# A transformer block stack on one core: the first mixer's columns in another order, and its selector's work in other places

## The chip, the cores and the metric

The kernel runs on one core of a Trainium2 chip. The metric is the device time of one execution in microseconds (us), median of repeated runs. PE is TensorE (its weight loads are PEld), DVE is VectorE, ACT is ScalarE, POOL is GpSimd, SP is the queue that issues the DMAs.

## What is computed

256 tokens of width 1024 pass two layers of a first kind (a SwiGLU network, a hybrid mixer, a SwiGLU network) and two of a second kind. The change touches the hybrid mixer only, which runs twice. One projection with 3792 columns feeds three attentions:

```python
proj = u @ w_in                     # 3792 columns, split into:
# aq ak av | iq ik iw | bq bk bv | cq ck cv | cf cg
aq, ak = rope(rms_norm(aq)), rope(rms_norm(ak))          # A: 4 heads, one shared key/value head
iq, ik = rope(iq), rope(ik)                              # selector: 8 heads, one key
score  = sum_h iw_h * scale * relu(iq_h . ik)            # causal
sel    = top_64(score)                                   # A attends to these keys only
bq, bk = rope(rms_norm(bq)), rope(rms_norm(bk))          # B: 4 heads, plain causal here (one block)
cq, ck = rms_norm(cq), rms_norm(ck)                      # C: 8 heads, forget gate
log_f  = log_sigmoid(cf + forget_bias)                   # cumulated over tokens, added to C's scores
o_c    = o_c * sigmoid(cg)
out    = concat(o_a, o_b, o_c) @ w_out
```

## The kernel before

Every engine runs a program written out by hand; semaphores join them. No planner is at work: what stands first in an engine's program runs first, and a waiting instruction holds all that stand behind it.

All weights come as a stream of parts of up to 128x2048 floats, three in flight. For each part ACT makes a rounded copy `w_hi` (`split_hi`, L330), which waits until the part three before it is used up, and DVE makes the rest `w_lo` (`split_lo`, L337). PE multiplies with both (L523 to L525).

In the first mixer (`mixer1`, written once for each engine) the 3792 columns are 15 parts, numbered m = 0 to 14: eight column groups g = 0 to 7, each of two halves in depth but for the last. `project_group` does a part for the first 128 tokens, then calls `within_part(m)`, does the second 128 tokens, and `after_part(m)` follows. So small work of the attentions stands between halves and parts of the projection. ACT and DVE have their own `within_part` and `after_part`, and their splits of part m + 3 stand in their `after_part(m)`. When a group is complete, `evacuate` (ACT, L1329) brings it from PSUM to `proj` (`proj_ready`).

The chain of the selector: POOL rotates its queries `I_Q` and key `I_K` (`rope1`, `rope_ready`), PE transposes them (`qk_turn`, L842), ACT copies them out (`qk_copy`, `qkT_ready`), PE multiplies (`index_scores`, L855, eight units u of two heads), ACT takes `relu(u)`, DVE weights and sums (`add_index(u)`, L1947, `idx_used`). `relu(u)` waits for `add_index(u - 2)`, since two buffers alternate. Then DVE searches in 8 rounds of `top_rounds` for each half of the tokens (L1962, L1963), and A's scores need the mask (`mask_ready`).

Norms of heads: ACT squares (`group_squares`, L1343), DVE sums (`head_means`, L1922, `gmean`), POOL takes the root (`group_roots`, L2316, `groot`), DVE scales (`scale_heads`, L1929; C's signal is `cqk_ready`) and, for A and B, applies gains (`gain_heads`, L1936, `normed`). The forget gate: DVE makes `z_abs`, ACT an exponential and a logarithm, DVE `log_f` (`logf_ready`), PE cumulates it (L912), ACT and DVE take it over (`forget_terms`).

The eight attention batches (C, C, A, B; two halves of tokens each) pass PE `scores(i)`, DVE `maxima(i)` (L1893), ACT `weights(i)` (L1313), PE `turn_p(i)` (L815), DVE `turned_p(i)`, PE `weigh(i)` (L826), DVE `weighed(i)` (`o_ready`). `turn_p(i)` also waits for `o_ready` of batch i - 1. At the end PE transposes the results (L702) and `project_out` multiplies by `w_out`.

## Time and profile before

| | |
|---|---|
| median of 3 runs | 1916.12 us (1915.83 to 1916.45) |
| the profiled execution | 1916.21 us, span of its trace 1914.1 us |
| PE busy | 1894.2 us, 99% |
| DVE, ACT, POOL busy | 1337.4, 968.3, 151.6 us |

Busy time on PE counts modelled ends, which reach over the next start: back to back, 128x512 matmuls start every 0.23 us but are shown with 0.39 us. An idle time in brackets is therefore a little shorter than what a wait takes from the flow of starts. A row's bracket names what ended the idle time before it.

### The profile page before, as it was taken

Reading aid. Unit: us, or ns where it says so; the run is one execution under the profiler, and the core shown is the slowest. Engines: PE = TensorE matmul, PEld = TensorE weight load, DVE = VectorE, ACT = ScalarE, POOL = GpSimd, SP = SyncE. Lnnn points to the kernel's source line nnn. Section 1 sums busy time; section 2 is a strip of 40 time slices with the busy share of each in tenths; the row PEclk is TensorE's granted clock in tenths of the full one; section 3 lists DMA queues with packets and bytes.
Section 4 is the critical chain, followed back from the end, with each engine's and each line's share of the span. In section 5 each row is a group of like instructions: output and inputs, shape, how many; then the busy total and the mean of one; then the engine's idle time right before and its main releaser. Section 6 shows DMA issues by size and latency. Waiting matters only on the chain.

```text
span 1914.1 us, 26132 instructions
## 1 busy us (share of the span) xinstructions
PE 1894.2 (99%) x10940; PEld 1639.4 (86%) x10940; DVE 1337.4 (70%) x1469; ACT 968.3 (51%) x1216; POOL 151.6 (8%) x158
## 2 busy tenths in 40 slices
PE   9999999999999999999999999999999999999998
PEld 7888878888888888788888888888888888888887
DVE  7887687787678766868776555569765654569763
ACT  5444565544444445555444565455444665455442
POOL 0000422100000005111000110000000110000000
PEclk9999999999999999999999999999999999999999
DMA  7655532455555555334545443444555443445552
GB/s 283 209 186 181 194 118 109 154 198 177 180 199 193 178 196 187 118 110 155 197 168 194 150 168 134 174 176 170 193 182 186 135 160 141 162 177 184 179 182 104
DMA packets 47491, 327.28 MB, mean 171 GB/s; under 512 B 5520, under 2 KB 5520, under 8 KB 11536
## 3 DMA queue, kind: packets, MB, share of 16 engines
q1 hardware_dynamic: 46512, 323.25, 47.4%
q10 hardware_dynamic: 864, 2.38, 0.3%
q8 instruction: 86, 1.41, 0.3%
q14 instruction: 29, 0.24, 0.0%
HBM read 324.56 MB, written 1.05 MB: 170 GB/s over the span
## 4 chain that ended last, share of the span: by engine, by line
PE 94%; DVE 3%; ACT 1%; issue 1%; POOL 1%; DMA 0%; DVEq 0%; POOLq 0%; ACTq 0%
PE ps L535 34%; PE ps L537 17%; PE ps L523 9%; PE ps L525 9%; PE ps L524 9%; PE ps L529 2%; PE ps L826 2%; PE ps L781 1%; PE ps L783 1%; PE ps L782 1%; PE ps L792 1%; PE ps L530 1%; PE ps L815 1%; DVE w_lo L337 1%; PE ps L550 1%
## 5 line engine op out<-in xcount | busy, mean ns | idle before, releaser
L330 ACT CAST w_hi<-raw 128x2048 fp32r<-128x2048 f32 (+3 forms) x314 | 580.2, 1849 | 581.9 <-PE ps L537 353.4
L337 DVE TENSOR_TENSOR w_lo<-raw,w_hi 128x2048 fp32r<-128x2048 f32 (+3 forms) x314 | 699.3, 2229 | 245.7 <-ACT w_hi L330 242.9
L535 PE MATMUL ps<-x_hl,w_hi 128*128 128x512 f32 x1968 | 494.2, 393 | 0.0
L535 PEld LDWEIGHTS ps<-x_hl,w_hi 128*128 128x128 f32 x1968 | 353.7, 189 | 63.6
L537 PEld LDWEIGHTS ps<-x_hl,w_lo 128*128 128x128 f32 x1968 | 268.5, 190 | 19.3
L537 PE MATMUL ps<-x_hl,w_lo 128*128 128x256 f32 x1968 | 274.4, 282 | 0.0
L523 PE MATMUL ps<-w_hi,x_hl 128*128 128x512 f32 (+3 forms) x672 | 262.0, 390 | 0.0
L525 PE MATMUL ps<-w_hi,x_hl 128*128 128x512 f32 (+3 forms) x672 | 254.2, 378 | 0.0
L524 PE MATMUL ps<-w_lo,x_hl 128*128 128x512 f32 (+3 forms) x672 | 253.5, 377 | 0.0
L1785 DVE TENSOR_REDUCE ffn_tmp<-ps 128x512 f32<-128x1024 f32 x132 | 161.3, 1223 | 103.5 <-PE ps L537 102.8
L535 PE MATMUL ps<-hid_hl,w_hi 128*128 128x512 f32 x836 | 212.9, 394 | 0.0
L535 PEld LDWEIGHTS ps<-hid_hl,w_hi 128*128 128x128 f32 x836 | 149.4, 188 | 26.9
L525 PEld LDWEIGHTS ps<-w_hi,x_hl 128*128 128x128 f32 x672 | 126.3, 188 | 23.5
L523 PEld LDWEIGHTS ps<-w_hi,x_hl 128*128 128x128 f32 x672 | 126.6, 188 | 22.3 <-issue 1.4
L524 PEld LDWEIGHTS ps<-w_lo,x_hl 128*128 128x128 f32 x672 | 126.7, 189 | 20.1
L2312 POOL TENSOR_TENSOR stat<-stat,const 128x2 f32<-128x2 f32 (+1 forms) x15 | 25.7, 1712 | 1448.9 <-DVE stat L1686 821.9
L537 PEld LDWEIGHTS ps<-hid_hl,w_lo 128*128 128x128 f32 x836 | 115.3, 188 | 10.3
L537 PE MATMUL ps<-hid_hl,w_lo 128*128 128x256 f32 x836 | 118.2, 282 | 0.0
L1201 ACT ACTIVATE x_hl<-h,gains 128x256 fp32r<-128x256 f32 x80 | 39.0, 507 | 91.3 <-DVE h L1868 78.4
L1242 ACT ACTIVATE ffn_tmp<-ffn_tmp 128x512 f32<-128x512 f32 x66 | 41.8, 633 | 71.1 <-DVE ffn_tmp L1791 70.8
L1245 ACT CAST hid_hl<-ffn_tmp 128x512 fp32r<-128x512 f32 x66 | 41.0, 621 | 25.0 <-DVE ffn_tmp L1796 24.1
L529 PE MATMUL ps<-x_hl,w_hi 128*128 128x512 f32 x144 | 51.5, 400 | 0.0
(286 smaller groups left out, 2198.4 us busy)
## 6 DMA issues: line engine op xcount, KB each, us to landing
raw<-in_parts SPq DMA_DIRECT2D x278, 1024.0 KB, 4.8
raw<-in_parts SPq DMA_DIRECT2D x20, 768.0 KB, 4.2
raw<-in_parts SPq DMA_DIRECT2D x4, 928.0 KB, 4.6
raw<-in_parts SPq DMA_DIRECT2D x4, 864.0 KB, 4.4
raw<-in_parts SPq DMA_DIRECT2D x6, 512.0 KB, 3.8
raw<-in_parts SPq DMA_DIRECT2D x4, 576.0 KB, 3.9
const<-in_const ACTq DMA_DIRECT2D x1, 1093.0 KB, 5.3
h<-in_x_t SPq DMA_DIRECT2D x1, 1024.0 KB, 7.6
```

Of the source, the lines that this page charges most:

```text
L330: nc.scalar.copy(w_hi[:, i % RING, 0:n_of(i)], raw[:, i % RING, 0:n_of(i)]).then_inc(high_ready, 1)
L337: nc.vector.tensor_tensor(w_lo[:, s, 0:n], raw[:, s, 0:n], w_hi[:, s, 0:n].bitcast(F32), ALU.subtract).then_inc(low_ready, 1)
L523: nc.tensor.matmul(out_, a_hi, b_hi, start=start, stop=False, skip_group_check=True)
L524: nc.tensor.matmul(out_, a_hi, b_lo, start=False, stop=False, skip_group_check=True)
L525: return nc.tensor.matmul(out_, a_lo, b_hi, start=False, stop=stop, skip_group_check=True)
L529: nc.tensor.matmul(ps[:, bank, :], w_h, hl.rearrange("p x n -> p (x n)"), start=start, stop=False, skip_group_check=True)
L535: nc.tensor.matmul(ps[:, bank, :], w_h(c), hl(c).rearrange("p x n -> p (x n)"), start=start and c == 0, stop=False, skip_group_check=True)
L537: m = nc.tensor.matmul(ps[:, bank, 0:SEQ], w_l(c), hl(c)[:, 0, :], start=False, stop=stop and c == kc - 1, skip_group_check=True)
L1201: nc.scalar.activation(x_hi(c), h[:, c, :], ACT.Copy, scale=gains[:, s, c:c + 1]).then_inc(xhi_ready, 1)
L1242: nc.scalar.activation(g_tmp, g_tmp, ACT.Silu).then_inc(silu_ready, 1)
L1245: nc.scalar.copy(hid_hl[:, p - 1:p + 1, 0, :], u_tmp.rearrange("p (f n) -> p f n", f=2)).then_inc(hidhi_ready, 1)
L1785: return nc.vector.tensor_reduce(dst.rearrange("p (f n) -> p f n", f=2), ps[:, b:b + 2, :].rearrange("p b (x n) -> p b n x", x=2), AX_X, A ...
```

## The change

The columns are laid out anew. Before, the groups were C_Q; I_Q; A_Q, A_K, A_V, I_K, I_W, C_F; C_K; C_V; B_Q, B_K; C_G; B_V. Now C_Q stands third: I_Q; A_Q to C_F; C_Q; C_K; C_V and so on. The work of the selector, of the norms and of the forget gate is placed to other parts accordingly on every engine, the search is spread as two rounds over each of eight places, and squares of heads go into a buffer of their own (`squares_early`) instead of `ffn_tmp`. Near the mixer's end the transposes of C's gated result come after `scores(5)` instead of ahead of it, and three small pieces stand one place earlier within `project_out`.

```diff
-MIX1 = (("C_Q", 1736, 512), ("I_Q", 384, 512), ("A_Q", 0, 256), ("A_K", 256, 64), ("A_V", 320, 64), ("I_K", 896, 64),
-        ("I_W", 960, 8), ("C_F", 3272, 8), ("C_K", 2248, 512), ("C_V", 2760, 512), ("B_Q", 968, 256), ("B_K", 1224, 256),
+MIX1 = (("I_Q", 384, 512), ("A_Q", 0, 256), ("A_K", 256, 64), ("A_V", 320, 64), ("I_K", 896, 64),
+        ("I_W", 960, 8), ("C_F", 3272, 8), ("C_Q", 1736, 512), ("C_K", 2248, 512), ...
-WIN1 = column_parts([512, 512, 464, 512, 512, 512, 512, 256])
+WIN1 = column_parts([512, 464, 512, 512, 512, 512, 512, 256])
...
-        QK_UNITS = [((12, 13), ("cqk_ready", 1), 0), ((14, 15), ("cqk_ready", 1), 1), ((3, 4), ("rope_ready", 1), 2),
-                    ((5, 6), ("rope_ready", 1), 3), ((7,), ("rope_ready", 2), 0), ((16, 17), ("cqk_ready", 2), 2),
-                    ((18, 19), ("cqk_ready", 2), 1), ((0, 1), ("rope_ready", 3), 3), ((2,), ("rope_ready", 3), 3),
+        QK_UNITS = [((3, 4), ("rope_ready", 1), 2), ((5, 6), ("rope_ready", 1), 3), ((7,), ("rope_ready", 2), 0),
+                    ((12, 13), ("cqk_ready", 1), 1), ((14, 15), ("cqk_ready", 1), 0), ((0, 1), ("rope_ready", 3), 1),
+                    ((2,), ("rope_ready", 3), 0), ((16, 17), ("cqk_ready", 2), 2), ((18, 19), ("cqk_ready", 2), 3),
```

PE, the new `within_part`, then `after_part`:

```diff
+                    if m == 5:
+                        qk_turn(2)
+                    if m == 6:
+                        index_scores(2, 3)
+                    if m == 7:
+                        index_scores(6, 7)
                     if m == 9:
                         pe.wait_ge(S["relu_ready"], 8)
                         qk_turn(7)
                         qk_turn(8)
+                    if m >= 10:
+                        turn_p(m - 10)
...
                     if m == 4:
                         qk_turn(0)
+                        qk_turn(1)
                     if m == 5:
+                        pe.wait_ge(S["qkT_ready"], 3)
+                        index_scores(0, 1)
                         pe.wait_ge(S["logf_ready"], 1)
...
+                    if m == 6:
+                        index_scores(4, 5)
+                    if m == 7:
+                        pe.wait_ge(S["aug_ready"], 2)
+                        qk_turn(3)
+                        pe.wait_ge(S["relu_ready"], 6)
+                        qk_turn(4)
+                    if m == 8:
+                        pe.wait_ge(S["qkT_ready"], 5)
+                        qk_turn(5)
+                        qk_turn(6)
                     if m == 9:
+                        pe.wait_ge(S["qkT_ready"], 9)
                         pe.wait_ge(S["aug_ready"], 3)
                         scores(0)
```

ACT, the new `after_part`:

```diff
+                    if m == 5:
+                        relu(0)
+                        relu(1)
+                    if m in (3, 5, 7):
                         act.wait_ge(S["proj_ready"], groups_of(WIN1)[m][0] + 1)
+                        group_squares(*{3: (A_Q, 320), 5: (C_Q, 512), 7: (C_K, 512)}[m], squares_early)
                     if m == 6:
                         relu(2)
                         relu(3)
                         forget_terms()
+                    if m == 7:
                         relu(6)
                         relu(7)
+                    split_hi(act, i0 + m + 3)
+                    if m == 7:
+                        qk_copy(3)
+                        qk_copy(4)
+                    if m == 8:
+                        qk_copy(5)
+                        qk_copy(6)
```

DVE, the new `within_part`, then `after_part`:

```diff
+                    if m == 7:
+                        scale_heads(proj[:, :, C_Q:C_Q + 512], 8).then_inc(S["cqk_ready"], 1)
                         add_index(4)
                         add_index(5)
+                    if 8 <= m <= 13:
+                        top_rounds(2)
...
+                    if m == 8:
+                        scale_heads(proj[:, :, C_K:C_K + 512], 8).then_inc(S["cqk_ready"], 1)
+                    if m >= 9:
+                        maxima(m - 9)
+                    if m == 12:
+                        step(scale_heads(proj[:, :, B_Q:C_G], 8))
...
                     if m >= 10:
                         weighed(m - 10)
                     split_lo(dve, i0 + m + 3)
+                    if m == 3:
                         step(scale_heads(proj[:, :, A_Q:A_V], 5))
                         gain_heads(proj[:, :, A_Q:A_V], 0, 4, 0)
+                    if m == 4:
                         step(nc.vector.memset(log_f, 0.0))
                         dve.wait_ge(S["ln_ready"], 2)
+                    if m == 5:
+                        add_index(0)
+                        add_index(1)
+                        head_means(8, squares_early)
+                    if m == 6:
                         add_index(2)
                         add_index(3)
                         forget_terms()
+                    if m == 7:
+                        head_means(8, squares_early)
+                        add_index(6)
+                        add_index(7)
+                    if m in (8, 9):
                         top_rounds(2)
```

POOL:

```diff
-                    group_roots(mdue, group_rs[:, 0:16])
-                    pool.wait_ge(S["proj_ready"], 2)
+                    pool.wait_ge(S["proj_ready"], 1)
                     for t in range(TT):
                         rope1(I_Q, 8, qk_i[:, t, 0:512], t)
...
-                    group_roots(mdue, group_rs[:, 0:10])
-                    pool.wait_ge(S["proj_ready"], 3)
+                    pool.wait_ge(S["proj_ready"], 2)
                     for t in range(TT):
                         rope1(I_K, 1, qk_i[:, t, 512:576], t)
                     nc.gpsimd.tensor_copy(qk_i[:, :, 576:640], qk_i[:, :, 512:576]).then_inc(S["rope_ready"], 1)
+                    group_roots(mdue, group_rs[:, 0:10])
                     pool.wait_ge(S["normed"], 2)
```

POOL's program at the start of the mixer, before (L2312 is the tokens' root, L2316 a root of heads, L2305 the first instruction of a rotation, L2343 the copy of the selector's key; the 128x512 rotation is I_Q, the 128x64 one I_K, the 128x320 one A_Q with A_K):

```order
L2312 TENSOR_TENSOR stat<-stat,const 128x2 [waits mean_ready]
L2316 TENSOR_TENSOR stat<-stat,const 128x16 [waits gmean,tables_in]
L2305 TENSOR_TENSOR arena<-arena,const 128x512 [waits proj_ready]
...
L2338 MEMSET pool_pad 128x1 [waits pool_step]
L2316 TENSOR_TENSOR stat<-stat,const 128x10 [waits gmean]
L2305 TENSOR_TENSOR arena<-arena,const 128x64 [waits proj_ready]
...
L2343 COPY arena<-arena 128x2x64 [waits pool_step]
L2305 TENSOR_TENSOR arena<-arena,const 128x320 [waits normed]
```

The same in the changed kernel, whose lines are about ten lower (L2306 is the root of heads, L2295 a rotation's first instruction):

```order
L2302 TENSOR_TENSOR stat<-stat,const 128x2 [waits mean_ready]
L2295 TENSOR_TENSOR arena<-arena,const 128x512 [waits proj_ready,tables_in]
...
L2327 MEMSET pool_pad 128x1 [waits pool_step]
L2295 TENSOR_TENSOR arena<-arena,const 128x64 [waits proj_ready]
...
L2331 COPY arena<-arena 128x2x64 [waits pool_step]
L2306 TENSOR_TENSOR stat<-stat,const 128x10 [waits gmean]
L2295 TENSOR_TENSOR arena<-arena,const 128x320 [waits normed]
...
L2306 TENSOR_TENSOR stat<-stat,const 128x16 [waits gmean,pool_step]
L2295 TENSOR_TENSOR arena<-arena,const 128x320
...
L2337 COPY arena<-arena 128x2x64 [waits pool_step]
L2306 TENSOR_TENSOR stat<-stat,const 128x16 [waits gmean] x2
```

The rotation of I_Q moved ahead of every root of heads and waits for the first group now; A's root (128x10) moved behind the rotation of I_K.

DVE's program from the means of C_K to its scaling, before (L1922 sums squares, L1929 scales, L1947 is `add_index`, L1962 a round of the search):

```order
L1922 TENSOR_REDUCE stat<-ffn_tmp 128x16 [waits gsq_ready]
L1923 TENSOR_SCALAR stat<-stat 128x16 [waits dve_step]
L337 TENSOR_TENSOR w_lo<-raw,w_hi 128x2048 [waits high_ready]
L1929 TENSOR_TENSOR arena<-arena,stat 128x512 [waits groot]
L1929 TENSOR_TENSOR arena<-arena,stat 128x512
...
L1947 SCALAR_TENSOR_TENSOR arena<-ffn_tmp,stat,arena 128x128 [waits dve_step]
L337 TENSOR_TENSOR w_lo<-raw,w_hi 128x2048 [waits high_ready,idx_used]
L1947 SCALAR_TENSOR_TENSOR arena<-ffn_tmp,stat,arena 128x128 [waits relu_ready]
...
L1947 SCALAR_TENSOR_TENSOR arena<-ffn_tmp,stat,arena 128x256 [waits dve_step]
L1893 TENSOR_REDUCE stat<-ps 128x4 [waits scores_done,idx_used]
L1947 SCALAR_TENSOR_TENSOR arena<-ffn_tmp,stat,arena 128x256 [waits relu_ready]
L1947 SCALAR_TENSOR_TENSOR arena<-ffn_tmp,stat,arena 128x256 [waits dve_step]
L337 TENSOR_TENSOR w_lo<-raw,w_hi 128x2048 [waits high_ready,idx_used]
L1962 MAX stat<-arena 128x8
```

The changed kernel from the split in `after_part(7)` to that in `after_part(8)` (L1915, L1922, L1940, L1955 in these roles):

```order
L337 TENSOR_TENSOR w_lo<-raw,w_hi 128x2048 [waits high_ready,idx_used]
L1915 TENSOR_REDUCE stat<-arena 128x16 [waits gsq_ready]
...
L1940 SCALAR_TENSOR_TENSOR arena<-ffn_tmp,stat,arena 128x256 [waits relu_ready,idx_used]
L1940 SCALAR_TENSOR_TENSOR arena<-ffn_tmp,stat,arena 128x256 [waits dve_step]
L1955 MAX stat<-arena 128x8 [waits idx_used]
L1956 MATCH_REPLACE arena<-stat,arena 128x128 [waits dve_step]
...
L1956 MATCH_REPLACE arena<-stat,arena 128x128 [waits dve_step]
L1922 TENSOR_TENSOR arena<-arena,stat 128x512 [waits groot,dve_step]
L1922 TENSOR_TENSOR arena<-arena,stat 128x512
L337 TENSOR_TENSOR w_lo<-raw,w_hi 128x2048 [waits high_ready]
L1955 MAX stat<-arena 128x8
```

C_K's scaling was the next thing but a split behind its means; four passes of `add_index` and two rounds of the search stand between now.

PE's program, before: units 0 to 3 of the selector, the cumulated forget gate (L912), then units 4 and 5 and the transposes of C_K (L842), with a half of a projection part at each "...":

```order
L855 MATMUL ps<-arena 128x128 [waits qkT_ready]
L855 MATMUL ps<-arena 128x128 x3
...
L855 MATMUL ps<-arena 128x128 [waits relu_ready,qkT_ready]
L855 MATMUL ps<-arena 128x128 x3
L912 MATMUL ps<-const,arena 128x256 [waits logf_ready]
L913 MATMUL ps<-const,arena 128x128
...
L855 MATMUL ps<-arena 128x256 [waits relu_ready]
L855 MATMUL ps<-arena 128x256 x3
L842 MATMUL ps<-const,arena 128x128 [waits cqk_ready,relu_ready]
L842 MATMUL ps<-const,arena 128x128 x3
```

The changed kernel: units 0 and 1 and the forget gate (L896) in `after_part(5)`; units 6 and 7 in `within_part(7)`; the transposes of C_K in `within_part(9)`:

```order
L856 MATMUL ps<-arena 128x128 [waits qkT_ready]
L856 MATMUL ps<-arena 128x128 x3
L896 MATMUL ps<-const,arena 128x256 [waits logf_ready]
L897 MATMUL ps<-const,arena 128x128
...
L856 MATMUL ps<-arena 128x256 [waits relu_ready]
L856 MATMUL ps<-arena 128x256 x3
...
L843 MATMUL ps<-const,arena 128x128 [waits cqk_ready,relu_ready]
L843 MATMUL ps<-const,arena 128x128 x3
L843 MATMUL ps<-const,arena 128x128 [waits cqk_ready]
L843 MATMUL ps<-const,arena 128x128 x3
```

The forget gate moved from `after_part(8)` to `after_part(5)`, and with the reordered columns C_K's transposes moved from between `within_part(9)` and `after_part(9)` to `within_part(9)` as a whole.

## Rows read from the trace of the kernel before

**Rows 1.** Sections 1 and 2 of the page: busy time, share of the span, instructions; the granted clock.

```profile
PE 1894.2 (99%) x10940; PEld 1639.4 (86%) x10940; DVE 1337.4 (70%) x1469; ACT 968.3 (51%) x1216; POOL 151.6 (8%) x158
...
PEclk9999999999999999999999999999999999999999
```

**Rows 2.** What TensorE waited for, whole program: us, times, longest us.

```profile
PE ps L815 <- ACT arena L1313: 6.3, 4, 1.7
```

**Rows 3.** TensorE's timeline, first mixer: start us, us, engine line op, count [idle before].

```profile
229.47 0.60 PE L842 MATMUL ps<-const,arena 128*128 128x128 f32 x4
...
235.38 1.03 PE L842 MATMUL ps<-const,arena 128*128 128x128 f32 x8
...
253.30 1.14 PE L855 MATMUL ps<-arena 64*128 64x256 f32 x8 [0.57 <-ACT ffn_tmp L1363]
...
265.98 0.63 PE L815 MATMUL ps<-const,arena 128*128 128x128 f32 x4 [1.65 <-ACT arena L1313]
...
308.80 1.17 PE L702 MATMUL ps<-const,rows 128*128 128x128 f32 x8 [0.29 <-DVE rows L2006]
```

**Rows 4.** Program's start: TensorE's timeline, then 8 to 12 us by windows (busy of PE, PEld, DVE, ACT, POOL; clock).

```profile
7.12 4.02 PE L550 MATMUL ps<-unsel 128*128 128x512 bf16 x10 [2.08 <-ACT w_hi L314]
...
8.00:12.00 4.00, 4.00 (x14) 2.13 (x13) 4.00 (x10) 3.87 (x11) 0.00 (x0) 0.63 1.01 428
```

**Rows 5.** GpSimd's timeline, first mixer, same columns.

```profile
220.45 1.12 POOL L2305 TENSOR_TENSOR arena<-arena,const 128x512 f32<-128x512 f32 x1 [4.85 <-ACT arena L1329]
...
222.74 2.67 POOL L2307 TENSOR_TENSOR arena<-arena 128x256 f32<-128x256 f32 x1
...
230.58 0.73 POOL L2307 TENSOR_TENSOR arena<-arena 128x256 f32<-128x256 f32 x1
...
232.07 0.10 POOL L2338 MEMSET pool_pad<- 128x1 f32 x1
232.85 1.97 POOL L2316 TENSOR_TENSOR stat<-stat,const 128x10 f32<-128x10 f32 x1 [0.69 <-DVE stat L1923]
...
237.51 0.36 POOL L2305 TENSOR_TENSOR arena<-arena,const 128x64 f32<-128x64 f32 x1
```

**Rows 6.** ScalarE's timeline, first mixer, same columns.

```profile
208.65 1.27 ACT L1329 ACTIVATE arena<-ps,stat 128x512 f32<-128x512 f32 x2 [4.38 <-POOL stat L2312]
...
237.57 1.28 ACT L1417 ACT_TABLE_LOAD   x1
...
243.49 1.15 ACT L1343 ACTIVATE ffn_tmp<-arena 128x512 f32<-128x512 f32 x2
...
248.55 1.90 ACT L330 CAST w_hi<-raw 128x2048 fp32r<-128x2048 f32 x1 [1.56 <-PE ps L525]
...
256.52 0.60 ACT L1363 ACTIVATE ffn_tmp<-ps 128x512 f32<-128x512 f32 x1 [2.33 <-DVE arena L1947]
```

**Rows 7.** VectorE's timeline, first mixer, same columns.

```profile
235.76 1.10 DVE L1929 TENSOR_TENSOR arena<-arena,stat 128x320 f32<-128x320 f32 x2
...
238.14 2.28 DVE L337 TENSOR_TENSOR w_lo<-raw,w_hi 128x2048 fp32r<-128x2048 f32 x1
240.42 0.27 DVE L2036 MEMSET arena<- 128x256 f32 x1
```

**Rows 8.** VectorE by line and form, first mixer: out<-in xcount, busy us, mean ns, idle.

```profile
L1929 DVE TENSOR_TENSOR arena<-arena,stat 128x512 f32<-128x512 f32 x6 | 5.0, 874 | 1.9 <-POOL stat L2316 1.9
L1893 DVE TENSOR_REDUCE stat<-ps 128x4 f32<-128x1024 f32 x4 | 4.9, 1218 | 0.0
...
L1922 DVE TENSOR_REDUCE stat<-ffn_tmp 128x16 f32<-128x1024 f32 x3 | 3.7, 1217 | 6.0 <-ACT ffn_tmp L1343 6.0
...
L1947 DVE SCALAR_TENSOR_TENSOR arena<-ffn_tmp,stat,arena 128x256 f32<-128x256 f32 x7 | 3.4, 483 | 1.9 <-ACT ffn_tmp L1363 1.7
...
L1936 DVE TENSOR_TENSOR arena<-arena,small 128x256 f32<-128x256 f32 x6 | 2.3, 430 | 0.1
...
L1962 DVE MAX8 stat<-arena 128x8 f32<-128x128 f32 x8 | 2.3, 291 | 0.2
```

More of the change, by code:

```diff
@@ L31 @@
 HD = 64
-MIX1 = (("C_Q", 1736, 512), ("I_Q", 384, 512), ("A_Q", 0, 256), ("A_K", 256, 64), ("A_V", 320, 64), ("I_K", 896, 64),
-        ("I_W", 960, 8), ("C_F", 3272, 8), ("C_K", 2248, 512), ("C_V", 2760, 512), ("B_Q", 968, 256), ("B_K", 1224, 256),
+MIX1 = (("I_Q", 384, 512), ("A_Q", 0, 256), ("A_K", 256, 64), ("A_V", 320, 64), ("I_K", 896, 64),
+        ("I_W", 960, 8), ("C_F", 3272, 8), ("C_Q", 1736, 512), ("C_K", 2248, 512), ("C_V", 2760, 512), ("B_Q", 968, 256), ("B_K", 1224, 256),
         ("C_G", 3280, 512), ("B_V", 1480, 256))
 MIX1_FROM = np.concatenate([np.arange(a, a + n) for _, a, n in MIX1])
-C_Q, I_Q, A_Q, A_K, A_V, I_K, I_W, C_F, C_K, C_V, B_Q, B_K, C_G, B_V = (
+I_Q, A_Q, A_K, A_V, I_K, I_W, C_F, C_Q, C_K, C_V, B_Q, B_K, C_G, B_V = (
     sum(n for _, _, n in MIX1[:i]) for i in range(len(MIX1)))
@@ L930, in after_part @@
                         pe.wait_ge(S["proj_ready"], 7)
+                        scores(5)
                         turn([(S["gated"], 1), (S["gated"], 2)], 4, mixed, o=4 * P, bank=4)
-                        scores(5)
                         qk_turn(9)
@@ L948, in mixer1, with turn_b0 @@
                 weigh(5)
-                project_out(i0 + 15, WOUT1, 1, stops={2: lambda: turn_p(6)})
-                turn([(S["o_ready"], 6)] * 2, 2, mixed, bank=3)
+                def turn_b0():
+                    turn_p(6)
+                    turn([(S["o_ready"], 6)] * 2, 2, mixed, bank=3)
+                project_out(i0 + 15, WOUT1, 1, stops={2: turn_b0})
                 scores(7)
@@ L960, in turn_b_rows @@
                     turn([(S["o_ready"], 8)] * 2, 2, mixed, o=2 * P, bank=2, singly=True)
-                project_out(i0 + 15, WOUT1, 2, 2, stops={4: turn_b1, 5: lambda: weigh(7), 7: turn_b_rows})
+                project_out(i0 + 15, WOUT1, 2, 2, stops={3: turn_b1, 4: lambda: weigh(7), 6: turn_b_rows})
                 project_out(i0 + 15, WOUT1, 3, 3, read=(h_ready, H_BEFORE[s]), singly=True)
@@ L1995, in within_part @@
                         turned_p(m - 10)
-                    if m == 12:
-                        top_rounds(2)
-                        step(scale_heads(proj[:, :, B_Q:C_G], 8))
-                        gain_heads(proj[:, :, B_Q:C_G], 0, 4, 2)
-                        gain_heads(proj[:, :, B_Q:C_G], 4, 4, 3)
                     if m == 14:
@@ L2041, in after_part @@
                         f.then_inc(S["logf_ready"], 1)
-                    if m == 7:
-                        scale_heads(proj[:, :, C_K:C_K + 512], 8).then_inc(S["cqk_ready"], 1)
-                    if m == 8:
+                    if m == 5:
[3 more added lines that the diff above has]
+                    if m == 6:
                         add_index(2)
```

119 lines of the change are left out of this document (28 added, 91 removed).

## The prediction

> **What bounds the kernel now.** I read the page first. TensorE is busy for 1894.2 of 1914.1 us, at the full clock in every slice [rows 1], so no other engine's busy time matters, and a change can only touch TensorE's pauses or make new ones. The reader should take from it how little there is to win: some 20 us, a part of it at the program's start. Next I read what TensorE waited for: the longest sum is 6.3 us in four pauses before `turn_p`, for the exponentials of ScalarE [rows 2]. Four pauses are two in each of the two mixers, so I work out one mixer and double it. Third, the timeline of the first mixer [rows 3]: before units 4 and 5 of the selector 0.57 us, released by a `relu`; before `turn_p(0)` 1.65 us; before the transposes of the gated result 0.29 us. With the second `turn_p` pause (6.3 / 2 - 1.65 = 1.5) the mixer holds 4.0 us. The part of 512 columns ending in the second row took 235.38 - 229.47 - 0.35 for its four transposes = 5.56 us, a half 2.8. Last, the other engines' timelines give what each step of a chain takes [rows 5 to 8].
>
> **What goes.** Batches start behind part 9 as before, but the selector's sums and the rounds are no longer all around them. By my replay below the exponentials of batch 0 end 0.2 us before TensorE wants them, so 0.57 and 1.65 go. At `turn_p(3)` the exponentials are in time too, and the 1.5 goes as such. The 0.29 goes, since `scores(5)` now fills it. Because a shown end reaches 0.15 us over the next start, four pauses are worth 4.0 + 0.6 = 4.6 us of starts. All matmuls stay; so do the DMAs, whose queue keeps its order (two narrower parts come earlier). The new buffer of the squares costs nothing: its space is `pT1`, first used in part 10.
>
> **What comes: the forget gate, part 5.** I use before's clock, on which the first group reaches `proj` at 208.65 + 1.27 = 209.9 [rows 6]. GpSimd can start on I_Q there instead of at 220.45. That rotation took from 220.45 to 232.07 = 11.6 us with two splits of VectorE in it [rows 5]; two fall into it again, so it ends at 221.6. I_K is eight instructions of up to 0.36 us and a copy, some 2.6 us, and a third split of 2.3 us starts just then: 226.5. Only now comes A's root, 1.97 us [rows 5]: 228.5. VectorE stands still for it since its split ended at 224.4, and behind A's scaling are queued the next split and the forget gate: from scaling to split 2.4, the split 2.3, then 1.4 [rows 7]: `logf_ready` at 234.6. ScalarE's share is ready by then: two table loads of 1.28 us and their functions [rows 6] and a third load end at 226.7, two copies and the high half at 229.6. TensorE ended parts 0 to 5 at 229.47 with four transposes; now with ten, so at 230.1, and after 0.85 for two units it stands before L896 at 230.95. **Wait 3.8 us**. If GpSimd were not held by the splits, ScalarE's 229.6 would decide, then 2.3 + 1.4 + 0.1: 233.4, a wait of 2.5; another held split gives 5. I take 3.8, which repeats the rotation's own row.
>
> A rule speaks here. The row shows one 128x256 instruction of GpSimd at 2.67 us beside a split, and the same at 0.73 us elsewhere [rows 5]. The Trainium skill (SBUF — State Buffer, the section on ports) says that the two engines share a port pair as an exclusive lock for a whole instruction; this case's trace agrees. With the lock the term is 3.8, without it 2.5.
>
> **The selector, part 7.** Units 6 and 7 want `relu(4)`, that wants `add_index(2)`, and that stands behind the split of part 9, which can't start before part 6 is used up. The row of a high half shows that it is TensorE that releases it [rows 6]. From the end of part 6: 0.2 + high half 1.9 + low half 2.3 + two passes 0.65 + relu 0.6 [rows 6 to 8] + 0.1 = 5.75. TensorE is there after units 4 and 5 (1.1) and half a part (2.9): 4.0. **Wait 1.75.** It is counted from a part's end, so a late TensorE does not shorten it.
>
> **C's queries and keys, parts 7 to 9.** From the end of part 7 ScalarE evacuates 1.3, squares 1.05, two relus 1.1 and then only makes the high half 1.9: 5.5 with the 0.2 of the signal. Two copies make 6.7, while TensorE is at the transposes behind part 8 after 0.75 + 5.6 = 6.4: **wait 0.3**. VectorE's low half ends at 7.8, C_K's means 1.3 (9.1), four passes of 0.5 (11.1), two rounds of four instructions in 1.4 (12.5), the scaling of C_K 1.3 (13.8) [rows 8]. TensorE is at C_K's transposes in `within_part(9)` after 6.4 + 0.3 + 0.5 + 2.9 = 10.1. **Wait 3.7.** The root of GpSimd (2.9 behind the means, 12.0) is hidden by passes and rounds.
>
> **Batches.** Counted from that wait's end: scores 0 are done at 5.0, VectorE has a split (2.3) and four rounds (1.4 each two) behind it at 5.1, the maxima and exponentials end at 7.4, TensorE comes at 7.6. Batches 1 and 2 keep margins of 0.2 us and more. In part 12 VectorE now takes maxima 1.2 [rows 8], B's scaling 1.3 and gains 1.4 and only then `weighed(2)` 0.6: 4.5 behind `scores(3)`, and `turn_p(3)` needs that `o_ready`. TensorE has 0.85 of `weigh(2)` and 2.85: **wait 1.0** with the signal.
>
> **The end.** `scores(5)` ahead of the transposes makes `project_out` wait for their split halves, up to 1.1 us more; three pieces placed earlier give back up to 0.8. I take +0.3, ends -0.8 and +1.1.
>
> **Sum for a mixer:** 3.8 + 1.75 + 0.3 + 3.7 + 1.0 = 10.55, less 4.6, plus 0.3: +6.25. Two mixers +12.5 us on the profiled execution's 1916.2 (its span 1914.1 and 2.1 around it; the median of the runs is 0.1 lower): 1928.7.
>
> **The clock.** At the start TensorE paused 2.08 us, and over the following 8 to 12 us its granted clock was 0.63, that is, partly at 1.2 instead of 2.4 GHz; after the pauses of 1.65 us it stayed at 1.00 [rows 1, 4]. The new waits of 3.8 and 3.7 us are longer than that 2.08, four in all. Those 4 us at 0.63 are 1.5 us of full clock lost in them alone, and the stretch may reach beyond them: a fall costs 1.5 to 1.75. None falling gives 0, all four 6.0 to 7.0. I take half, 3.3: **1932.0 us**. The Trainium skill (TensorE: Matmul & The Clock Gate, Part 1) says that idleness takes the clock to its lower level and activity brings it back; the start's row agrees. With that rule at every long pause the sum would be about 1935, without it 1928.7.
>
> **Rivals.**
> - *The lead carries over* (faster). If the first long wait gave ScalarE and VectorE a lead, so that the splits of parts 9 and 10 were done before TensorE needs what stands behind them, the 1.75, 0.3 and 3.7 would vanish, and with the least forget gate wait a mixer would be 2.5 + 1.0 - 4.6 = -1.1: 1914.0. For it: VectorE is idle for a third of the time. Against: the high half waits for TensorE's part end [rows 6], whatever lead there is. It decides when the three fall below 1.1 us in sum. Chance 0.06.
> - *The waits cancel the gains* (no change): both long waits at about half, 2.0, because the splits hold GpSimd less and the passes overlap: 2.0 + 1.0 + 2.0 + 0.3 - 4.6 = 0.7, some 1917.6. Chance 0.06.
> - *Mild:* the forget gate at 2.5, C_K at 3.0, the end at -0.3, no fall of the clock: a mixer +3.6, 1923.4. For it: each is a lower bound of a row. Chance 0.2.
> - *The pauses before `turn_p` stay* (the change does not do what it says): the margin at `turn_p(0)` is 0.2 us; one more held VectorE instruction per part would bring 1.65 and 1.5 back on top: +6.3, and with the clock 1938. Chance 0.15.
> - *My forecast*, 1926 to 1936, has 0.53.
>
> **Chances and range.** Faster by over 0.2% (3.8 us, about what a measurement of this kernel tells from no change) 0.06, within 0.2% 0.06, slower by more 0.88. The range runs from 1922, just under the mild case, to 1939: it leaves out the two first rivals and little above.
>
> **What the changed profile would show.** Right: in each mixer a pause of 3 to 5 us before L896, of 1.5 to 2 before L856 with 256 columns, of 3 to 4 before L843 in part 9, about 1 before the fourth L816, released by VectorE; none before the first L816. Wrong: if L896 comes without a pause, GpSimd's root of ten columns must have ended by 225; if L843 in part 9 does, C_K's scaling came before the passes. A clock below 1.00 behind the long pauses tells how much of the last 3.3 us is real.

## The result, and the profile after

The changed kernel takes 1936.09 us (median of 4 runs, 1934.82 to 1936.75), the one before 1916.28 in the same comparison: ratio 1.0102, 95% interval 1.0085 to 1.0120. It is slower, by 19.8 us; 1932.0 was predicted. The profiled execution took 1936.75 us, its span is 1934.7.

The page of the changed kernel, TensorE's busy time and its clock in 40 slices, then the view of the core with its mean granted clock:

```profile
PE 1901.6 (98%) x10937; PEld 1644.0 (85%) x10940; DVE 1336.2 (69%) x1469; ACT 968.1 (50%) x1216; POOL 159.2 (8%) x158
...
PEclk9999999999999999999999999999999999999999
...
core 0: 1934.7 us, clock 0.995
```

With the same matmuls TensorE is busy for 7.4 us longer than before [rows 1]. Work that did not grow takes longer only if it runs slower, so already the page says that a part of the loss is the clock. Its 40 slices don't show it: each is 48 us long, and all read 9. The mean granted clock does, 0.995 against 0.999 before.

TensorE's waits in the changed kernel (us in total, times, longest). Lines have shifted: L843, L856, L816 and L896 are the former L842, L855, L815 and L912.

```profile
PE ps L843 <- DVE arena L1922: 7.5, 2, 3.7
PE ps L896 <- DVE arena L2026: 5.6, 2, 2.8
PE ps L856 <- ACT ffn_tmp L1356: 4.2, 2, 2.1
PE ps L816 <- DVE rows L1900: 2.0, 2, 1.0
...
PE ps L843 <- ACT arena L1347: 1.3, 2, 0.6
```

The wait that led the list before, `turn_p` for ScalarE's exponentials, 6.3 us [rows 2], is gone. Five others stand there, each twice, once a mixer: 20.6 us (and 0.3 for C's copies). The first mixer in TensorE's timeline:

```profile
233.64 0.70 PE L896 MATMUL ps<-const,arena 128*128 128x256 f32 x2 [2.82 <-DVE arena L2026]
...
248.61 1.14 PE L856 MATMUL ps<-arena 64*128 64x256 f32 x8 [2.11 <-ACT ffn_tmp L1356]
...
259.22 0.87 PE L843 MATMUL ps<-const,arena 128*128 128x128 f32 x6 [0.15 <-ACT arena L1345]
...
266.59 1.94 PE L843 MATMUL ps<-const,arena 128*128 128x128 f32 x8 [3.73 <-DVE arena L1922]
...
276.85 0.60 PE L816 MATMUL ps<-const,arena 128*128 128x128 f32 x4
...
304.89 1.07 PE L816 MATMUL ps<-const,arena 128*128 128x128 f32 x8 [0.98 <-DVE rows L1900]
...
322.11 0.66 PE L843 MATMUL ps<-const,arena 128*128 128x128 f32 x4 [0.64 <-ACT arena L1347]
```

These are the places that [rows 3] showed before: the relus of 0.57, `turn_p(0)` of 1.65 (now the row at 276.85, without a pause) and the gated transposes of 0.29 wait no more. In their place come the forget gate (2.82), units 6 and 7 (2.11), C's copies (0.15), C_K's transposes (3.73), block 2's division (0.98) and the last turn of q and k (0.64). The transposes at 266.59 took 1.94 us, those of the same form 1.03 before [rows 3].

Windows of 2 us of the same stretch (busy of PE, PEld, DVE, ACT, POOL, then the granted clock):

```profile
232.00:234.00 2.00, 0.36 (x2) 0.33 (x3) 1.52 (x6) 2.00 (x4) 1.92 (x4) 1.00 0.38 66
234.00:236.00 2.00, 2.00 (x9) 1.61 (x8) 1.11 (x1) 0.86 (x1) 0.49 (x2) 0.65 0.98 414
236.00:238.00 2.00, 2.00 (x6) 1.59 (x5) 1.93 (x4) 0.00 (x0) 0.00 (x0) 0.50 0.11 45
...
264.00:266.00 2.00, 0.00 (x0) 0.00 (x0) 1.86 (x8) 0.00 (x0) 0.89 (x1) 0.83 0.25 102
266.00:268.00 2.00, 1.41 (x7) 1.44 (x8) 2.00 (x2) 0.28 (x1) 0.00 (x0) 0.50 0.00 0
```

Behind the pause of 2.82 us the clock goes to 0.50, which is 1.2 instead of 2.4 GHz. A matmul of 128x512 then starts every 0.43 us, where one starts every 0.23 us at the full clock:

```profile
235.09 0.63 PE L526 MATMUL ps<-w_hi,x_hl 128*128 128x512 f32 x1
235.52 0.63 PE L524 MATMUL ps<-w_hi,x_hl 128*128 128x512 f32 x1
```

Summed over all windows of 2 us (window times one less its clock) the execution lost 10.2 us of full clock in the mixers, in five places at or behind pauses. The one before lost 2.6 by the same sum, none of it in the mixers, 1.7 at the program's start and the rest at its end. Not all of the 10.2 us is lost time: at C_K the clock fell while TensorE still stood in its pause (window 264 to 266, clock 0.83, no matmul).

Why the gate waits: GpSimd, then VectorE, then ScalarE, of the changed kernel.

```profile
211.96 2.67 POOL L2297 TENSOR_TENSOR arena<-arena 128x256 f32<-128x256 f32 x1
...
215.40 3.05 POOL L2295 TENSOR_TENSOR arena<-arena,const 128x512 f32<-128x512 f32 x1
...
225.92 1.96 POOL L2306 TENSOR_TENSOR stat<-stat,const 128x10 f32<-128x10 f32 x1
```

```profile
227.92 0.89 DVE L1922 TENSOR_TENSOR arena<-arena,stat 128x320 f32<-128x320 f32 x2 [3.60 <-POOL stat L2306]
...
229.79 2.29 DVE L337 TENSOR_TENSOR w_lo<-raw,w_hi 128x2048 fp32r<-128x2048 f32 x1
...
232.76 0.83 DVE L2026 TENSOR_SCALAR arena<-stat 128x16 f32<-128x16 f32 x3
...
261.65 2.04 DVE L1940 SCALAR_TENSOR_TENSOR arena<-ffn_tmp,stat,arena 128x256 f32<-128x256 f32 x4
...
265.15 1.29 DVE L1922 TENSOR_TENSOR arena<-arena,stat 128x512 f32<-128x512 f32 x2
```

```profile
227.41 1.92 ACT L330 CAST w_hi<-raw 128x2048 fp32r<-128x2048 f32 x1
```

The root of A ends at 227.88, VectorE has stood still for 3.60 us, and scaling, gains, split and `log_f` follow until 233.6. The high half that this split needs was ready at 229.33, 0.46 us before the split began; so an earlier root would have brought `log_f` at most 0.5 us sooner. The last two of VectorE's rows are C_K's side: the sums of units 6 and 7, then two rounds of the search, and only then the scaling.

### The profile page after: what moved, and what is told of

Its sections match the earlier page's. It is cut to its first block, busy times and chain, and to the rows that moved or that the text cites. A ratio compares the mean times of both kernels' runs of the same rounds, so it can differ in the third digit from the quotient of the medians.

```text
span 1934.7 us, 26125 instructions
## 1 busy us (share of the span) xinstructions
PE 1901.6 (98%) x10937; PEld 1644.0 (85%) x10940; DVE 1336.2 (69%) x1469; ACT 968.1 (50%) x1216; POOL 159.2 (8%) x158
## 4 chain that ended last, share of the span: by engine, by line
PE 91%; DVE 4%; POOL 2%; ACT 2%; issue 1%; DMA 0%; DVEq 0%; POOLq 0%; SPq 0%; ACTq 0%
PE ps L536 34%; PE ps L538 17%; PE ps L524 9%; PE ps L526 9%; PE ps L525 9%; PE ps L827 1%; PE ps L530 1%; PE ps L793 1%; PE ps L782 1%; PE ps L784 1%; PE ps L783 1%; DVE w_lo L337 1%; PE ps L816 1%; ACT w_hi L330 1%; PE ps L531 1%
## 5 line engine op out<-in xcount | busy, mean ns | idle before, releaser
L337 DVE TENSOR_TENSOR w_lo<-raw,w_hi 128x2048 fp32r<-128x2048 f32 (+4 forms) x314 | 700.2, 2232 | 267.5 <-ACT w_hi L330 264.8
L330 ACT CAST w_hi<-raw 128x2048 fp32r<-128x2048 f32 (+4 forms) x314 | 580.4, 1849 | 590.8 <-PE ps L538 351.3
L524 PE MATMUL ps<-w_hi,x_hl 128*128 128x512 f32 (+3 forms) x672 | 265.4, 395 | 0.0
L526 PE MATMUL ps<-w_hi,x_hl 128*128 128x512 f32 (+3 forms) x672 | 257.0, 382 | 0.0
L525 PEld LDWEIGHTS ps<-w_lo,x_hl 128*128 128x128 f32 x672 | 128.4, 191 | 20.6
```

Source lines behind the costliest of these rows:

```text
L330: nc.scalar.copy(w_hi[:, i % RING, 0:n_of(i)], raw[:, i % RING, 0:n_of(i)]).then_inc(high_ready, 1)
L337: nc.vector.tensor_tensor(w_lo[:, s, 0:n], raw[:, s, 0:n], w_hi[:, s, 0:n].bitcast(F32), ALU.subtract).then_inc(low_ready, 1)
L524: nc.tensor.matmul(out_, a_hi, b_hi, start=start, stop=False, skip_group_check=True)
L525: nc.tensor.matmul(out_, a_hi, b_lo, start=False, stop=False, skip_group_check=True)
L526: return nc.tensor.matmul(out_, a_lo, b_hi, start=False, stop=stop, skip_group_check=True)
```

## The experiments

All times are medians; 1916 is the kernel before on the same chip (1915.98 to 1916.2). Unless said otherwise a kernel is the changed one with one edit and computes all of the reference.

**fill: the pauses kept, the clock held up.** Idle matmuls, whose result nobody reads, stand ahead of the three long pauses; nothing else moves.

```diff
                         index_scores(0, 1)
+                        warm_up(12)
                         pe.wait_ge(S["logf_ready"], 1)
...
+                        pe.wait_ge(S["relu_ready"], 4)
+                        warm_up(8, 2)
                         index_scores(6, 7)
...
                         pe.wait_ge(S["relu_ready"], 8)
+                        warm_up(16, 2)
                         qk_turn(7)
```

> The changed kernel with idle matmuls (128x512 of an unused tile into a bank that is free) on TensorE ahead of its three long pauses: 12 before the forget gate, 8 before units 6 and 7, 16 before C_K's transposes. No pause is shortened and no other engine's work moves. Theory (pauses plus clock): the pauses stay as sums of matmuls and idle time, but the granted clock no longer falls behind them. The profile of the changed kernel shows a mean clock of 0.995 over 1934.7 us, 9.7 us of full clock lost, some 2 of them inside the pauses themselves: 1936.1 - 7 = about 1929, clock 0.998 or more. Rival (the clock's falls are harmless, the pauses alone make the 20 us): 1936, whatever the clock. Rival 2 (idle matmuls overrun the pauses): over 1936.

Measured: 1928.33 us (1928.29 to 1928.80), ratio 1.0064 [1.0047, 1.0080]. Its timeline (L551 are the idle ones):

```profile
230.90 2.76 PE L551 MATMUL ps<-unsel 128*128 128x512 bf16 x12
...
261.66 3.63 PE L551 MATMUL ps<-unsel 128*128 128x512 bf16 x16
...
265.49 1.09 PE L843 MATMUL ps<-const,arena 128*128 128x128 f32 x8 [0.20 <-DVE arena L1926]
```

The real work behind them still waits for the same releasers as before the edit, yet no window of the mixers is below 1.00, and 7.8 us are gone: the theory, not the rival with 1936. So of the 19.8 us lost, 7.8 are the clock and 12.0 the waits less the removed pauses: the prediction's sum for those, without clock, was 1928.7.

**gate: the gate's cumulation taken in later.** TensorE does it (the wait and its two matmuls) behind units 2 and 3 in the middle of part 6.

```diff
                         index_scores(0, 1)
-                        pe.wait_ge(S["logf_ready"], 1)
-                        upto_all = const[:, CONST_AT["upto"][0]:CONST_AT["upto"][0] + SEQ]
...
                     if m == 6:
                         index_scores(2, 3)
+                        pe.wait_ge(S["logf_ready"], 1)
+                        upto_all = const[:, CONST_AT["upto"][0]:CONST_AT["upto"][0] + SEQ]
...
```

> The changed kernel with the cumulated forget gate taken by TensorE behind units 2 and 3 in within_part(6) instead of behind units 0 and 1 in after_part(5). Theory: the pause of 2.8 us goes, since log_f is there at 233.6 and TensorE comes at about 234.5, and with it the fall of the clock behind it (1.7 us of work); VectorE and ScalarE then have less lead for the selector's sums, which gives back about 1 us: 3.5 us a mixer, 1929. Rival (what is late is the selector's chain, and the pause only moves to units 4 to 7 at its full size): 1934 to 1936.

Measured: 1934.84 us (1933.47 to 1937.17), ratio 1.0099. TensorE's timeline of this run:

```profile
238.25 1.13 PE L856 MATMUL ps<-arena 64*128 64x256 f32 x8 [0.42 <-ACT ffn_tmp L1356]
...
245.53 2.08 PE L856 MATMUL ps<-arena 64*128 64x256 f32 x8 [3.19 <-ACT ffn_tmp L1356]
```

The pause of 2.82 is gone, and 1.1 and 0.4 come back at the selector's relus. Only 1.3 us a mixer of the pauses are won, and of the clock nothing: each 3.19 brought it down as each 2.82 had, and by the window sum the mixers lost 10.2 us of full clock as before the edit. The theory (1929) fell. The rival had the time (1934 to 1936) and the place to which the pause moves, but not the size: 1.5 of 2.82 us moved, not all.

**forget: the same pause removed at its source.** VectorE makes `log_f` (the whole block, five instructions) ahead of A's scaling, while it has nothing to do.

```diff
                     split_lo(dve, i0 + m + 3)
+                    if m == 3:
+                        step(nc.vector.memset(log_f, 0.0))
+                        dve.wait_ge(S["ln_ready"], 2)
...
                     if m == 3:
                         step(scale_heads(proj[:, :, A_Q:A_V], 5))
...
-                    if m == 4:
-                        step(nc.vector.memset(log_f, 0.0))
-                        dve.wait_ge(S["ln_ready"], 2)
...
```

> The changed kernel with one block moved on VectorE: the forget gate's log_f is computed behind weight part 3 and ahead of the scaling of A, instead of behind weight part 4. In the trace of the changed kernel ScalarE has the logarithm at 225.05 us, VectorE then stands still until 227.88 for GpSimd's root, and the block is 0.8 to 1.5 us long, so it fits into that idle time. Theory (the wait at the cumulated gate is one of the order in VectorE's queue, root and scaling and split ahead of log_f): the pause of 2.8 goes in each mixer, and the 3.4 us of half clock behind it in each: 1936.1 - 5.6 - 3.4 = 1927. Rival (TensorE only arrives earlier at the relus of units 2 and 3, whose sums stand behind VectorE's split, as when the gate was taken later): the pause of 2.1 there grows to 4 or so, 1931 to 1934.

Measured: 1934.24 us (1933.47 to 1937.16), ratio 1.0096. VectorE, then TensorE:

```profile
225.18 0.33 DVE L2022 TENSOR_SCALAR arena<-stat 128x16 f32<-128x16 f32 x3
...
227.63 0.90 DVE L1922 TENSOR_TENSOR arena<-arena,stat 128x320 f32<-128x320 f32 x2 [2.12 <-POOL stat L2306]
```

```profile
245.46 2.08 PE L856 MATMUL ps<-arena 64*128 64x256 f32 x8 [3.19 <-ACT ffn_tmp L1356]
```

`log_f` is there 8 us sooner, and the time is that of `gate`. The rows show that the gate's pause is one of order in VectorE's queue; that its removal alone brings 9 us is refuted. The rival had the place right, with 3.19 instead of about 4. Both runs leave the same chain: VectorE's sums of units 2 and 3 behind its split.

**sums: units 2 and 3 ahead of the split.**

```diff
                 def after_part(m):
+                    if m == 6:
+                        add_index(2)
+                        add_index(3)
                     split_lo(dve, i0 + m + 3)
...
                     if m == 6:
-                        add_index(2)
-                        add_index(3)
                         forget_terms()
```

> The changed kernel with VectorE's passes of add_index(2) and (3) ahead of the split in after_part(6) instead of behind it. Theory: units 6 and 7 wait for relu(4), that for these passes, and these for the split of part 9, so the pause of 2.1 us before units 6 and 7 goes: 2 x 2.2 = 4.4 us and the one fall of the clock that followed it in the second mixer, 1930. Rival (the pause comes from ScalarE, which takes the relus behind its own high half of part 9): the pause shrinks by less than 1 us, 1934 or more.

Measured: 1928.50 us (1928.17 to 1929.02), ratio 1.0065. TensorE in this run:

```profile
249.96 1.06 PE L843 MATMUL ps<-const,arena 128*128 128x128 f32 x8 [0.44 <-DVE arena L1922]
...
263.37 1.94 PE L843 MATMUL ps<-const,arena 128*128 128x128 f32 x8 [3.46 <-DVE arena L1922]
```

The pause of 2.11 is gone, 0.44 comes back at C_Q's transposes in the first mixer, and by the window sum the mixers lose 5.1 us of full clock instead of 10.2. The 7.6 us won are about 4 of pauses (C_K's was 0.27 shorter here) and the rest clock. That rest is not all due to the edit: of the two places where a fall is gone, one is units 6 and 7, the other the gate in the first mixer, whose pause of 2.8 us the edit left as it was. And behind C_K's pause in the first mixer the low stretch was half as long.

**keys: C_K's chain.** Its means go ahead of the split of part 7, its scaling right behind that split, ahead of the sums and rounds.

```diff
+                    if m == 7:
+                        head_means(8, squares_early)
                     split_lo(dve, i0 + m + 3)
...
                     if m == 7:
-                        head_means(8, squares_early)
+                        scale_heads(proj[:, :, C_K:C_K + 512], 8).then_inc(S["cqk_ready"], 1)
                         add_index(6)
...
-                    if m == 8:
-                        scale_heads(proj[:, :, C_K:C_K + 512], 8).then_inc(S["cqk_ready"], 1)
```

> The changed kernel with VectorE's means of C_K ahead of the split in after_part(7) and C_K's scaling right behind that split, ahead of add_index(6), (7) and of two rounds of the search. Theory: cqk_ready comes at 9.1 us behind the end of part 7, TensorE at 10.2, so the pause of 3.7 us goes with the falls of the clock behind it: 2 x 3.9 + 1.7 + 2.8 = 12.3, 1924. Rival (VectorE's load is the limit, and what is taken ahead is missing behind): a new pause at the first turn_p of 2 us or more, 1928 to 1932.

Measured: 1928.46 us (1926.91 to 1929.90), ratio 1.0064. TensorE, then VectorE:

```profile
271.81 0.66 PE L816 MATMUL ps<-const,arena 128*128 128x128 f32 x4 [1.82 <-ACT arena L1306]
```

```profile
269.53 0.69 DVE L1886 TENSOR_REDUCE stat<-ps 128x4 f32<-128x512 f32 x1
```

The 3.73 at C_K is gone and 1.82 stands at `turn_p(0)`: TensorE brings the first scores sooner, and VectorE takes their maxima only behind a split and four rounds. Half of the gain moved on, as the rival said, whose pause (2 us or more) was a little too long; its 1928 to 1932 holds, the theory's 1924 does not.

**search: two of those rounds moved behind the maxima.** `keys`, with the two rounds of `within_part(9)` behind the split of `after_part(9)`.

```diff
-                    if 8 <= m <= 13:
+                    if 8 <= m <= 13 and m != 9:
                         top_rounds(2)
...
                     if m in (8, 9):
-                        top_rounds(2)
+                        top_rounds(2 if m == 8 else 4)
```

> The run 'keys' with one more thing moved: two of the selector's search rounds go from ahead of the first maxima to behind the split of that part (four there, none ahead). 'keys' had a pause of 1.82 in each mixer ahead of the first turn of P, with the maxima behind split and four rounds at 269.53. Theory (VectorE's order there made the pause): the maxima come 1.44 earlier, the pause shrinks to 0.4 or less, 1928.5 - 2.8 = 1925.6, and down to 1924 where half clock goes with it. Rival (the mask, then 1.4 later, holds up the copy of the turned P and with it the first weighed sum): a new pause of 0.5 to 1.5 ahead of L827, 1927 to 1929.

Measured: 1925.45 us (1923.64 to 1925.72), ratio 1.0046. TensorE's timeline, then its clock (windows):

```profile
233.95 0.70 PE L896 MATMUL ps<-const,arena 128*128 128x256 f32 x2 [2.81 <-DVE arena L2026]
...
247.79 1.13 PE L856 MATMUL ps<-arena 64*128 64x256 f32 x8 [2.57 <-ACT ffn_tmp L1356]
...
270.01 0.65 PE L816 MATMUL ps<-const,arena 128*128 128x128 f32 x4 [0.39 <-ACT arena L1306]
```

```profile
234.00:236.00 2.00, 2.00 (x10) 1.73 (x11) 0.81 (x1) 1.16 (x1) 0.80 (x2) 1.00 0.92 369
```

The 1.82 is 0.39, and no pause ahead of the weighed sums appeared; 0.46 did at the next turn of P. The windows show something else: the same pause of 2.8 us at the gate as in the changed kernel, and this time the clock stays at 1.00 behind it. The next pause, at units 6 and 7, is then 2.57 us instead of 2.11. In the profiled executions of the changed kernel, `keys`, `search` and `weighed`, which have this wait unedited, it is 2.57 in the four mixers without a fall at the gate and 2.11 or 2.12 in the four with one. So a fall at the gate costs less in the end than its slow matmuls: the next wait gives back 0.46 us.

**weighed: block 2's division ahead of B's scaling.**

```diff
                     if m == 12:
+                        weighed(2)
                         step(scale_heads(proj[:, :, B_Q:C_G], 8))
...
-                    if m >= 10:
+                    if m >= 10 and m != 12:
                         weighed(m - 10)
```

> The changed kernel with VectorE's division of block 2 taken ahead of the scaling of B in part 12 (what the kernel before did). Theory (the two scalings, 2.7 us, stand ahead of it since the change): the wait of 1.0 for o_ready at the fourth turn of P goes in each mixer: 1936.1 - 2.0 = 1934.1. Rival (B's scaled heads are then late for the last two turns of q and k, which already wait 0.64): that wait grows by as much, 1936.

Measured: 1933.66 us (1932.02 to 1935.55), ratio 1.0094. The wait of 0.98 is not in its trace, the 0.64 is as it was: the theory, though the 2.4 won are no more than the spread of these runs.

**every: all the moves that removed a pause** (`forget`, `sums`, `search` with `keys`, `weighed`).

> The changed kernel with all the moves that take away a pause of their own: log_f ahead of A's scaling, the sums of units 2 and 3 ahead of the split, C_K's means and scaling around the split of part 7, the search rounds of 'search', and block 2's division ahead of B's scaling. Theory (the pauses are independent and together with the half clock behind them the whole loss): 1936.1 - 2 x (2.8 + 2.1 + 3.7 + 1.0) = 1916.9, less 7.8 for the clock as in 'fill' = 1909, plus 1 to 3 for what is left: 1910 to 1912, below the kernel before. Rival (VectorE is full in these stages; each pause taken away only brings TensorE sooner to the next wait for it): 1916 to 1921.

Measured: 1912.17 us (1911.58 to 1913.04, 10 runs), ratio 0.9978 [0.9969, 0.9987]: 4 us below the kernel before. TensorE's waits in it:

```profile
PE ps L843 <- DVE arena L1922: 2.7, 2, 1.3
...
PE ps L843 <- ACT arena L1347: 1.3, 2, 0.6
PE ps L856 <- ACT ffn_tmp L1356: 0.9, 2, 0.4
...
PE ps L816 <- ACT arena L1306: 0.7, 2, 0.4
```

The mixers' waits fell from 20.6 to 5.6 us, and the clock in them is 1.00 throughout. The result lies 0.2 us above the theory's 1910 to 1912 and well below the rival's 1916 to 1921. The theory's premise holds only in part: the pauses are not independent, for 1.33 us now stand at C_Q's transposes in each mixer, where `sums` had 0.44 in one.

**end: `every` with the former end of the parts** (the gated result's transposes ahead of `scores(5)`).

> The run 'every' with the end of the parts as the kernel before had it: the transposes of C's gated result ahead of scores(5), not behind. Theory (the change's order of the end costs 0.64 at the last turn of q and k, since its copy waits for the split halves of the transposed result on ScalarE, and saves the 0.29 that the transposes waited for the gated rows): 0.64 - 0.29 = 0.35 in each mixer, so 1912.2 - 0.7 = 1911.5. Rival (the 0.3 that the prediction took for the end was spent in the projection out, which the halves reach later or earlier): within 0.3 of 1912.2, or slower by up to 1.

Measured: 1912.86 us (1912.37 to 1913.38, 11 runs), ratio 0.9983: 0.7 above `every` (0.9 against the kernel before on each run's own chip), the other way than the theory, and within the rival's bound. TensorE's timeline of this run:

```profile
309.64 0.65 PE L843 MATMUL ps<-const,arena 128*128 128x128 f32 x4 [0.22 <-ACT arena L1347]
311.07 0.36 PE L782 MATMUL ps<-m_hl,w_hi 128*128 128x256 f32 x1 [0.78 <-DVE m_hl L1738]
```

The 0.64 shrinks to 0.22, but `project_out` now waits 0.78 for VectorE's half of the transposed result. Together 1.00 instead of 0.64 a mixer, 0.7 in both. So within `every` this part of the change is right by 0.36 us a mixer.

**most: `every` with C_Q's scaling ahead of the forget gate's casts.**

> The run 'every' with C_Q's scaling on VectorE taken from behind the forget gate's three casts to ahead of them, right behind the one instruction that reads the cumulated gate. In 'every' it stands at 247.00 and TensorE waits 1.33 for it at the transposes of C_Q in each mixer. Theory (its place in VectorE's queue makes that pause; GpSimd's root for it ends at 244.0): it starts at 245.06, 1.9 earlier, the pause goes: 1912.2 - 2.7 = 1909.5. Rival (the sums of units 4 and 5, now behind the casts as before but with the scaling 1.3 to 1.6 long unchanged ahead, or ScalarE's copies behind them, hold up the next turns): 1911 to 1912.

Measured: 1912.07 us (1911.30 to 1912.74, 11 runs), ratio 0.9979: no gain that can be told from `every`. TensorE and VectorE of this run:

```profile
253.86 0.88 PE L843 MATMUL ps<-const,arena 128*128 128x128 f32 x6 [0.63 <-ACT arena L1345]
```

```profile
244.42 2.10 DVE L1922 TENSOR_TENSOR arena<-arena,stat 128x512 f32<-128x512 f32 x2
```

The 1.33 is gone; 0.63 stands at the next transposes, which wait for ScalarE's copies, and a second wait for the exponentials appears. The scaling itself takes 2.10 us where it took 1.61 in `every` and 1.29 in the changed kernel. That is the rival, whose 1911 to 1912 is missed by less than 0.1.

## Why the prediction was right, and what was sized wrong

The verdict, the range and the mechanism held: new waits of VectorE's and GpSimd's chains outweigh the removed pauses. The point forecast was 4.1 us low, and 1936.09 lies just above the 1926 to 1936 that the prediction called its own forecast. Of its signs, two waits came outside their bounds: 2.82 at the gate (3 to 5 was said) and 2.11 at units 6 and 7 (1.5 to 2). Point by point, for one mixer:

- *What goes.* 4.6 us of starts were to go with the pauses of the relus, both `turn_p` and the gated transposes. None of them is in the trace of after, so the fourth rival ("the pauses before `turn_p` stay") is out; the exponentials of batch 0 ended 0.3 us before TensorE came, 0.2 was predicted.
- *The forget gate:* 3.8 predicted (its own times, 234.6 less 230.95, give 3.65), 2.82 measured. The replay was right in kind: the rotation ran beside two splits (an instruction of 2.67 us where [rows 5] have 0.73 without one, and one of 3.05 where they have 1.12), VectorE stood still for the root and then did scaling, split and gate in that order. It ended at 233.6 instead of 234.6: the rotation was through 0.5 sooner (221.1), and scaling with gains took 1.87 instead of 2.4. The Trainium skill's rule on the ports (SBUF — State Buffer, the section on ports) was the step that chose 3.8 over 2.5; by that rule, the trace agrees, for GpSimd's held instructions stand beside splits again. But the hold decided little here: with the high half ready at 229.33, it made the wait at most 0.5 us longer, and 2.82 lies nearer to the 2.5 than to the 3.8.
- *Units 6 and 7:* 1.75 predicted, 2.11 measured. `relu(4)` began 1.23 us behind the start of the passes (246.73 to 247.96), where 0.65 was taken for two of them: GpSimd rotated A beside them. And the wait is not quite fixed by the part's end, as the prediction had it: it is 2.57 where no fall of the clock came before.
- *C's copies* 0.3 against 0.15, *C_K* 3.7 against 3.73, *block 2's division* 1.0 against 0.98.
- *The end:* +0.3 as a net term; the trace shows 0.64 at the last turn of q and k, which I had not seen (its copy stands behind ScalarE's split halves), and no wait at `project_out`, where I had put up to 1.1. Two small waits that stand in no term nearly cancel: the kernel before waited 0.46 in `project_out`, the changed one does not, and it waits 0.39 behind the mixer. Before, then after:

```profile
341.43 0.36 PE L781 MATMUL ps<-m_hl,w_hi 128*128 128x256 f32 x1 [0.46 <-DVE m_hl L1745]
```

```profile
362.59 2.11 PE L536 MATMUL ps<-x_hl,w_hi 128*128 128x512 f32 x8 [0.39 <-DVE w_lo L337]
```

- *The sum.* The predicted waits of a mixer are 10.55 and 0.3 for the end, the measured 10.43 with the 0.64. Errors of both signs cancelled, and that is luck. The comparison also flatters a little: the predicted waits are differences of starts, the measured ones brackets, which by the 0.15 us of each would be 11.3. `fill` measures the whole part: 1928.33 against 1928.7.
- *The clock:* this is the term that was mis-sized. I took 3.3 us, half of the highest case, from 0 to 7; `fill` shows 7.8. Three things in the step failed. I let half of the four long pauses bring the clock down; in the profiled execution all four did. I counted only these four as candidates, but the 2.11 of units 6 and 7 brought it down too, in the second mixer. And a fall lasted longer behind the 3.73 in the first mixer (the windows from 264 to 274 lose 3.4 us of full clock) than the 1.75 that I took for one from the program's start. With 7.8 the sum is 1936.5; 1936.09 was measured, which says no more than that `fill` came 0.4 below its 1928.7. The sentence on the rule "at every long pause", which gave about 1935, was nearer than my half.

The rivals on the fast side fell for the reason given: the high half is released by TensorE's end of a part, so no lead carried over. `gate` and `forget` agree with that: TensorE reached units 6 and 7 3.1 us sooner there (245.5 against 248.6), so most of the chain had moved ahead with it, and the wait did not shrink but grew, from 2.11 to 3.19.

What the experiments add is where the loss came from: not the column order by itself, but the places on VectorE's program. The same order with a few blocks of that program moved runs 24 us faster than the change as made, and 4 us faster than the kernel before. That the new order is what wins these 4 us is not shown: no run tried such moves in the old order. Not settled: why a pause of 2.8 us costs the clock in one execution and not in another (below), and how the 2.4 us of `weighed` divide.

## What to carry to other kernels

When work is moved ahead on the engine that bounds, replay each helper engine's queue in its written order, from the event that releases it; the pauses predicted so were right to 0.4 us, but for one. Test a pause by removing it and looking where it comes back: of the gate's pause and of C_K's about half came back at the next wait, and only the whole set beat the start. And price a pause of two us or more on TensorE with the slow matmuls behind it, not only with its length; idle matmuls put into the pauses measure that price in one run.

## What the runs showed of the hardware

Whether the clock falls goes with the pause's length, and below 3 us also with something that these runs don't show. I counted in the profiled executions of all kernels whether a window behind a pause shows 0.50. Pauses of 3.2 to 3.8 us in the mixers: 14 of 14. Of 2.8 us: 5 of 10, and the same place fell in one mixer and not in the other of the same execution (`sums`, `keys`, `weighed`). Of 2.1 to 2.6: 3 of 8. Of 1.8 (`keys`): 1 of 2. Of 1.5 to 1.7, as before the change: 0 of 4. At the program's start, with other work before the pause, it fell behind 2.08 us [rows 4], 2.23 (`every`) and 2.31 (`search`), and not behind the nine pauses of 1.4 to 1.9. The spread of the runs fits: 0.5 us between the lowest and the highest for `fill`, which has no fall, 3.7 for `gate` and `forget`. These two have no pause that falls only at times, but the length of a fall differed: in their profiled executions 1.7 us of full clock lost in each place of the first mixer, 3.4 in each of the second. In the second mixer of the changed kernel the clock fell behind 2.11 us:

```profile
780.69 2.08 PE L856 MATMUL ps<-arena 64*128 64x256 f32 x8 [2.11 <-ACT ffn_tmp L1356]
...
780.00:782.00 2.00, 1.31 (x6) 1.13 (x8) 1.85 (x6) 1.19 (x2) 0.15 (x1) 0.68 0.72 262
```

The Trainium skill (TensorE: Matmul & The Clock Gate, Part 1) says that idleness lowers the clock and steady work restores it. Both are seen here; that the same pause need not lower it twice is what the runs add.
